# Down projection on fp16 pairs, scaled by powers of two per tile and unit, with a third copy of its weights

## The reference

```python
FFN_HIDDEN = ((8 * D_MODEL + 3 * 256 - 1) // (3 * 256)) * 256      # 2816, 22 tiles of 128

def swiglu(h, w_gate, w_up, w_down):
    return (jax.nn.silu(h @ w_gate) * (h @ w_up)) @ w_down

x = x + ga_f * swiglu(modulate(rms_norm(x, g_ffn), sh_f, sc_f), w_gate, w_up, w_down)
```

## Time and profile before

| | us |
|---|---|
| median of 3 runs | 1775.1 (1769.41 to 1775.48) |
| the profiled execution | 1775.53 |
| its span, first to last instruction | 1773.7 |
| TensorE busy | 1669.4 (94%) |
| VectorE busy | 962.2 (54%) |
| GpSimd busy | 784.9 (44%) |
| ScalarE busy | 662.7 (37%) |
| mean granted TensorE clock | 0.979 of full |

### The profile page before, as it was taken

The page is one execution under the profiler, slowest core; times in us unless marked ns, Lnnn a source line. Parts: engine busy times, 40 slices in busy tenths (PEclk is TensorE's granted clock), DMA queues, the critical chain, the costliest instruction groups (busy, mean ns, idle before and its releaser), DMA issues.

```text
span 1773.7 us, 27789 instructions
## 1 busy us (share of the span) xinstructions
PE 1669.4 (94%) x10959; PEld 1230.3 (69%) x10959; DVE 962.2 (54%) x1715; ACT 662.7 (37%) x1218; POOL 784.9 (44%) x576
## 2 busy tenths in 40 slices
PE   7999989978989999999899999997988999999998
PEld 3688878867856678666776687886776645645647
DVE  3534499895468851686418844457996522112112
ACT  3222378874143220333013113226875354153130
POOL 2144445653524452345414342551334558368363
PEclk9999999999989999999999998998999899999999
DMA  9345453313134513344225422654003224333332
GB/s 318 49 117 142 124 136 93 90 49 86 34 95 123 151 60 95 96 140 145 65 78 176 148 69 48 148 130 109 16 1 95 72 77 124 86 103 99 83 84 83
DMA packets 317279, 179.11 MB, mean 101 GB/s; under 512 B 88526, under 2 KB 310494, under 8 KB 317150
## 3 DMA queue, kind: packets, MB, share of 16 engines
q1 hardware_dynamic: 284542, 143.63, 30.9%
q10 hardware_dynamic: 32608, 33.71, 6.1%
HBM read 158.97 MB, written 2.83 MB: 91 GB/s over the span
## 4 chain that ended last, share of the span: by engine, by line
PE 60%; DVE 5%; POOL 2%; issue 2%; ACT 2%; SPq 1%; DMA 1%; ACTq 0%; DVEq 0%; POOLq 0%
PE acc L892 55%; PE small L1168 1%; DVE act L1619 1%; DVE stat L1781 1%; DVE prob_t L1795 1%; DVE scaled_ffn L1633 1%; POOL split_w L656 1%; SPq L534 1%; PE side L1073 1%; ACT prob_t L1420 0%; POOL pair_w L764 0%; PE mod_ps L989 0%; DMA inv_rows<-inv_row 0%; PE side L882 0%; DVE o_sum L1807 0%
## 5 line engine op out<-in xcount | busy, mean ns | idle before, releaser
L892 PE MATMUL acc<-act,pair_w 128*128 128x512 f16 x3168 | 580.5, 345 | 7.3 <-ACT act L1284 4.2
L892 PEld LDWEIGHTS acc<-act,pair_w 128*128 128x128 f16 x3168 | 307.5, 98 | 270.1 <-DVE act L1619 10.1
L892 PE MATMUL acc<-act,split_w 128*128 128x512 f32 (+1 forms) x1920 | 376.4, 354 | 9.9 <-DVE act L1881 4.6
L892 PEld LDWEIGHTS acc<-act,split_w 128*128 128x128 f32 x1920 | 306.4, 189 | 63.1 <-DVE act L1881 6.8
L892 PE MATMUL acc<-hidden,split_w 128*128 128x512 f32 (+1 forms) x1584 | 310.4, 357 | 10.7 <-issue 6.3
L892 PEld LDWEIGHTS acc<-hidden,split_w 128*128 128x128 f32 x1584 | 261.9, 190 | 56.6 <-issue 7.1
L653 POOL TENSOR_SCALAR split_w<-raw_w 128x1024 fp32r<-128x1024 f32 (+1 forms) x120 | 125.6, 1047 | 383.0 <-PE acc L892 292.8
L656 POOL TENSOR_TENSOR split_w<-raw_w,split_w 128x1024 fp32r<-128x1024 f32 (+1 forms) x120 | 279.2, 2327 | 10.0
L761 POOL TENSOR_SCALAR pair_raw<-pair_raw,weight_scale 128x1024 f32<-128x1024 f32 x88 | 106.1, 1205 | 357.9 <-ACT pair_w L1469 357.9
L1944 DVE SCALAR_TENSOR_TENSOR mod_acc<-mod_chunk,silu_c,mod_acc 128x256 f32<-128x256 f32 x280 | 228.1, 857 | 4.0
L1644 DVE SCALAR_TENSOR_TENSOR x_t<-acc,mod,x_t 128x512 f32<-128x512 f32 x96 | 60.3, 658 | 253.6 <-PE acc L892 253.1
(11 more groups left out here) (188 smaller groups left out, 1837.0 us busy)
## 6 DMA issues: line engine op xcount, KB each, us to landing
mod_chunk<-in_w_mod ACTq DMA_DIRECT2D x28, 1024.0 KB, 5.4
pair_raw<-in_w_gate SPq DMA_DIRECT2D x44, 512.0 KB, 4.0
pair_raw<-in_w_up SPq DMA_DIRECT2D x44, 512.0 KB, 5.4
raw_w<-in_w_in SPq DMA_DIRECT2D x64, 256.0 KB, 3.8
raw_w<-in_w_down SPq DMA_DIRECT2D x32, 512.0 KB, 3.9
raw_w<-in_w_mod SPq DMA_DIRECT2D x24, 512.0 KB, 4.1
mod_start<-in_w_mod SPq DMA_DIRECT2D x8, 1024.0 KB, 12.2
ks<-q_split SPq DMA_DIRECT2D x64, 96.0 KB, 2.3
```

Source lines behind the costliest of these rows:

```text
L892: mm = pe.matmul(acc[slot][:, a:b], weights[:, part == 2, k, :], moving[:, part == 1, k, a:b], start=(k == 0 and part == 0), stop=(k == n ...
```

## The change

The down projection goes over to fp16 pairs. Its weights get their own three raw buffers (`down_raw`), four pairs (`down_w`) and four `down_low`, a third fp16 copy: the raw scaled weight times 2^-11, which multiplies the low half of `hidden` in place of the high weights. `hidden` becomes fp16. Each down unit r = (layer, chunk, j) has a power of two of its own from the sum of squares of its tile, and each hidden tile a share (`hid_share`) from the scales of its gate and up weights; the residual's gate takes them back (`down_gate`). In a chunk's last three f the units 0, 1, 2 are prepared; unit j+3 is squared and scaled in unit j. The bound of the activations takes the maximum of the gains over partitions in place of their sum, with a transpose on TensorE.

```diff
+                def split_down(ch, j):
+                    r, n = n_down(l, ch, j), CHUNKS[ch]
+                    pool.wait_ge(down_scaled, r + 1)
+                    if r >= 4:
+                        pool.wait_ge(unit_done, u_of_down(r - 4) + 1)
+                    pool.tensor_scalar(down_low[r % 4][:, 0:n, :], down_raw[r % 3][:, 0:n, :], 2.0 ** -11, 0.0, ALU.mult, ALU.add)
+                    pool.wait_ge(down_hi, r + 1)
+                    pool.tensor_tensor(down_w[r % 4][:, 1, 0:n, :], down_raw[r % 3][:, 0:n, :], down_w[r % 4][:, 0, 0:n, :],
+                                       ALU.subtract).then_inc(down_ready, 1)
...
-                    for j in range(KT):
-                        split(u_down(l, ch) + j, n)
...
+                    split_down(ch, 0)
+                    for j in range(1, KT):
+                        if f0 + n < FT and j in (1, 2):
+                            split_pair(f0 + n + j - 1, 0)
+                        split_down(ch, j)
+                        if f0 + n < FT and j in (1, 2):
+                            split_pair(f0 + n + j - 1, 1)
...
+            def sum_down(r):
+                pe.wait_ge(down_sq, r + 1)
+                if r:
+                    pe.wait_ge(down_bits, r)
+                high = down_sum[:, r % 4:r % 4 + 1].bitcast(BF16)[:, 1:2]
+                pe.matmul(side[:, 0:1], ones16[:, :], high, start=True, stop=True).then_inc(down_ps, 1)
...
+                        if f >= f0 + n - 3:
+                            sum_down(n_down(l, ch, f - (f0 + n - 3)))
...
-                        pe.wait_ge(split_ready, ring_of[u] + 1)
+                        pe.wait_ge(down_ready, r + 1)
                         pe.wait_ge(resid, 32 * l + KT * (ch + 1) + j - 1)
+                        def down_tile(k):
+                            if j == 0:
+                                hidden_tile(k)
+                            if k == n - 1 and j + 3 < KT:
+                                sum_down(r + 3)
...
+                def square_down(ch, j, l=l):
+                    r, n = n_down(l, ch, j), CHUNKS[ch]
+                    sc.wait_ge(down_in[r % 3], 16 * (r // 3 + 1))
...
+                def round_down(ch, j, l=l):
+                    r, n = n_down(l, ch, j), CHUNKS[ch]
+                    sc.wait_ge(down_scaled, r + 1)
...
+                def last_downs(k):
+                    if k >= 1 and k + 2 < KT:
+                        round_down(len(CHUNKS) - 1, k + 2)
+                    if k + 3 < KT:
+                        square_down(len(CHUNKS) - 1, k + 3)
...
                         if f + 2 < FT:
                             square_pair(f + 2)
+                        if f >= f0 + n - 3:
+                            square_down(ch, f - (f0 + n - 3))
...
                         if f + 2 < FT:
                             round_pair(f + 2)
+                        if f >= f0 + n - 3:
+                            round_down(ch, f - (f0 + n - 3))
+                    if ch < len(CHUNKS) - 1 or l == DEPTH - 1:
+                        for j in range(3, KT):
+                            square_down(ch, j)
+                            round_down(ch, j)
...
+                def scale_down(ch, j):
+                    ve.wait_ge(down_ps, r + 1)
...
+                    ve.scalar_tensor_tensor(out=raw, in0=raw, scalar=down_scale[:, 2:3],
+                                            in1=hid_share[:, 0:n].rearrange("p (k a) -> p k a", a=1).broadcast_to((P, n, P)),
+                                            op0=ALU.mult, op1=ALU.mult).then_inc(down_scaled, 1)
...
                         product(f)
+                        if f == f0 + n - 3:
+                            share_hidden(ch)
+                        if f >= f0 + n - 3:
+                            scale_down(ch, f - (f0 + n - 3))
...
-                            residual(j % 2, x_t[:, j, :], l, mod[:, l, 5 * KT + j, :], w)
+                            residual(j % 2, x_t[:, j, :], l, down_gate[:, n_down(l, ch, j) % 4, :], w)
+                            if j + 3 < KT:
+                                scale_down(ch, j + 3)
```

More of the change, by code:

```diff
@@ L303, in trunk @@
         prod = place("prod", [P, TOK], F32, c0 + 3072)
+        down_raw = [place("down_raw0", [P, 8, P], F32, b0 + 24576)] + raw_w
+        down_low = [place(f"down_low{i}", [P, 8, P], F16, where)
+                    for i, where in enumerate((b0 + 28672, b0 + 30720, c0 + 10240, c0 + 12288))]
+        down_w = [place(f"down_w{i}", [P, 2, 8, P], F16, b0 + 32768 + 4096 * i) for i in range(4)]
+        squares_down = place("squares_down", [P, 8 * P], BF16, norm_at + 2 * 4 * TOK)
         squares_out = place("squares_out", [P, 8 * P], BF16, c0 + 22528)
@@ L403, in trunk, with n_down, u_of_down @@
             ring += [(u_out(ll) + j, 6) for j in range(KT)]
-            ring += [(u_down(ll, ch) + j, 1) for ch in range(len(CHUNKS)) for j in range(KT)]
         ring_of = {u: r for r, (u, _) in enumerate(ring)}
+        def n_down(l, ch, j):
+            return (l * len(CHUNKS) + ch) * KT + j
+        def u_of_down(r):
+            return u_down(r // (len(CHUNKS) * KT), r // KT % len(CHUNKS)) + r % KT
         def landed(u):
@@ L630, in _ @@
                         load_pair(f)
-                    for j in range(KT):
+                        if f == f0 + n - 2:
+                            for j in range(3):
+                                load_down(ch, j)
+                    if f0 + n < FT:
+                        load_pair(f0 + n)
+                        load_pair(f0 + n + 1)
+                    for j in range(3, KT):
                         load_down(ch, j)
-                        if j < 2 and f0 + n < FT:
-                            load_pair(f0 + n + j)
             for t in range(4):
@@ L891, in dense_tile @@
                     for a, b in ((0, 512), (512, TOK))[:1 if w == LAT else 2]:
-                        mm = pe.matmul(acc[slot][:, a:b], weights[:, part == 2, k, :],
+                        own = low[:, k, :] if low is not None and part == 1 else weights[:, part == 2, k, :]
+                        mm = pe.matmul(acc[slot][:, a:b], own,
                                        moving[:, part == 1, k, a:b],
@@ L1298, in _ @@
                 sc.activation(root_first[:, :], eps[:, 0:1], ACT.Sqrt)
-                squares(2 * l, TOK, ready)
+                squares(2 * l, TOK, ready, last_downs if l else None)
                 def take_rows(i):
```

124 lines of the change are left out of this document (92 added, 32 removed).

## The result

The changed kernel takes 1813.0 us (median of 4 runs, 1811.3 to 1814.2); the kernel before, beside it, 1774.7 us (4 runs). The ratio is 1.0221, 95% interval 1.0199 to 1.0244: slower by some 39 us. The forecast was 1808 us, range 1783 to 1832.

The account below looks back on a forecast made before the run. TensorE, busy 94% of 1773.7 us, bounds the kernel. Rests of +10.9 (layer 0) and +15.4 (layer 1), clock +5, sums +1.4 make +32.7 on 1775.5, the 22.8 gain already inside: 1808 us, range 1783 to 1832.

Parts of the forecast that it names:

- (a): Likeliest case: TensorE waits for the added scaling and square chain in both layers' down phases; 1808 us, 70%.
- The format's gain: Down matmuls in fp16: 11.0 us less in layer 0, 6.4 in layer 1, 5.4 from four buffers; together -22.8.
- The chain per unit: Down units 1 to 4, residual to square: layer 1 short by 0.6 us, its last chunk by 1.1; layer 0 passes.
- Unit 1 of layer 0: TensorE waits for the square's sum before unit 1's last tile; first chunk rests 8 us, until 658.8.
- Unit 0 of layer 0: Sum for unit 3 in down unit 0: rest of 3.7 us forecast in layer 1's first chunks, none in layer 0.
- The scaling: VectorE's scaling of a 128x1024 down tile: 1.2 us taken, bounds 0.96 and 3.3 if it meets a GpSimd subtraction.
- rival (d): VectorE's scaling and GpSimd's subtraction collide in most chains, costing 2 us more in each of those units: 1838 us, 12%.
- Silu in layer 1: First two chunks: ScalarE, held at the rounding of unit 0, gives silu late to the next gate; 2.2 us each.
- The clock: Lower clock behind TensorE's rests: 2.8 us per layer 0 chunk, 5 in all for layer 1, bounds 0 and 14.
- Costed at nothing: Semaphores, maximum for the bound, later sums, extra scale operations, weight loads lie beside TensorE's work; layer 1's attention part: 0.

Follow-up runs that it names:

- e10_fp16_spread: e6_fp16_alone, with the late-modulation sums of the last f of layer 0's first two chunks spread over down units 0 to 3: 1742.8 us, 0.9832.
- e6_fp16_alone: Kernel before, with down weights and `hidden` as unscaled fp16 pairs made by GpSimd, two buffers, no third copy: 1757.3 us, 0.9906.
- e1_ahead: Changed kernel, with ScalarE's square of down unit r+1 put ahead of its rounding of unit r: 1787.2 us, 1.0088.
- e3_both: e1_ahead, with the sums of even and odd down units in two PSUM banks: 1782.5 us, 1.0065.
- e7_spread: e3_both, with the late-modulation sums of each layer 0 chunk's last f spread over down units 0 to 3: 1768.3 us, 0.9969.
- e5_const: Changed kernel without squares and sums for the down units, each scaled by the same constant power of two: 1777.7 us, 1.0033.
- e9_after_spread: Changed kernel, with the late-modulation sums of each layer 0 chunk's last f spread over down units 0 to 3: 1790.4 us, 1.01.
- e11_later_add: e8_all, with TensorE's last late-modulation sum in layer 0 after down unit 5 instead of 4, VectorE's addition behind residual 6: 1758.0 us, 0.9922.
- e8_all: e7_spread, with ScalarE's roundings of down units 0 and 1 moved behind silu, each one f later: 1766.7 us, 0.9962.

## Why the prediction was right, step by step

The forecast is 5 us under the measurement, and its likeliest case, (a), is what happened: the chain residual, small operations, scaling, rounding, square, sum reaches round to TensorE's own queue. That it came so close is in part errors that cancel. On the span, layer 0's down phases cost 5.1 us more than forecast (16.0 against 10.9), layer 1's three chunks 3.0 less (17.4 against 15.4 and 5 for the clock), everything else 1.8 more (3.2 against 1.4).

- *The format's gain* was right in the stream: a down unit takes 7.8 us in layer 0; layer 1's last down phase is 31.3 us in e10_fp16_spread against 33.0, 1.8 less (forecast 1.9). All of it together, 22.8 us, is never seen: e6_fp16_alone gives 17, since the two rests on GpSimd per layer 1 chunk stay with two buffers (0.93 and 1.18 us) and layer 0's late residual takes some. The kernel as changed has the four buffers, and in its place the other rests.
- *The chain per unit.* Forecast short by 0.6 us in layer 1 and 1.1 in the last chunk; measured 0.39 and 0.99. The 1.6 us for unit 1 in layer 1 did not come in either chunk, the 1.3 for unit 2 only in the first (1.26, then 0.40), so a chunk's rests are 6.4 and 5.5 us and not 7.8. Layer 0's later units pass, as forecast.
- *Unit 1 of layer 0.* Sum forecast at 658.8, came at 658.23. This closeness is luck. The phase began 1.7 us earlier than in the kernel before (634.44 instead of 636.10), so counted from its start the sum came 23.8 us in and not 22.7; the scaling ahead of the late sums took 3.18 us and not 1.2. The forecast's own terms, too, put the residual at 653.1 (653.04 + 2.25 - 2.15) and not at 653.6. The cause of the rest has three parts, by experiment: the square behind the rounding (e1_ahead: the rest goes from 6.81 to 5.05), the single PSUM column (e3_both: to 3.99), the late sums in front of the residual (e7_spread: to none).
- *Unit 0 of layer 0* is the term that was missing. I counted it for layer 1 alone (3.7, measured 4.36), but the sum for unit 3 also rests 2.01, 2.57 and 3.84 us in layer 0's three chunks. This is the main part of the 5.1 us that the three chunks came out above the forecast. Not all of the 8.4 us adds, since unit 1's rest ends when VectorE is through, whenever it began (6.81 us instead of 8).
- *The scaling* was the disputed price: 1.2 taken, 0.96 to 3.3 as bounds. It is 1.28 alone, up to 3.18 when it meets a subtraction, mean 1.79. This made unit 0's chain long in layer 0's first two chunks (3.18 us at 638.03 and at 844.32) and, with the two-column operation of 1.97 us, in layer 1's (1.88 at 1518.62). In layer 0's third chunk it is 1.02 us for six tiles; there the last product itself stood behind late sums until 1016.69. The 32 large scalings together took 16 us more than without collisions, not all of them in a chain that TensorE waits for, and rival (d), 1838 us, did not come.
- *Silu in layer 1*: forecast 2.2 us a chunk; the gate/up phases of the first two chunks are 2.0 us longer. ScalarE is late as forecast, held by VectorE's scaling (2.61 us at 1495.53), but TensorE meets this first at the square's sum (0.86 us at 1502.60) and then at silu (0.48 at 1503.26), before the gate unit of the chunk's last f.
- *The clock.* I gave 2.8 us to each chunk of layer 0 and 5 in all to layer 1. The windows of the changed kernel (us, busy of TensorE, of its loads, of VectorE, ScalarE and GpSimd, granted clock, DMA) behind the rests of 2.01, 6.81, 4.36 (twice) and 2.46 us:

```profile
643.43:650.98 7.55, 7.55 (x48) 4.58 (x49) 7.55 (x10) 0.00 (x0) 4.58 (x3) 1.00 0.25 69
...
658.23:663.20 4.97, 4.97 (x17) 2.34 (x18) 2.70 (x7) 0.00 (x0) 1.11 (x1) 0.50 0.37 106
...
1522.73:1529.60 6.87, 6.87 (x25) 2.76 (x26) 2.97 (x6) 2.10 (x3) 6.79 (x4) 0.75 0.27 76
...
1658.20:1665.10 6.90, 6.90 (x21) 2.63 (x22) 3.42 (x6) 1.85 (x2) 6.82 (x4) 0.62 0.26 76
1767.70:1771.80 4.10, 4.07 (x19) 1.69 (x19) 2.33 (x6) 0.76 (x2) 1.50 (x2) 1.00 0.33 96
```

  Of the rests in layer 1 the two of 4.36 us cost something, that of 2.46 us nothing: 6.87 x 0.25 and 6.90 x 0.38, 4.3 us. In layer 0 the losses are 2.5 (4.97 x 0.5), about 2.8 and, in the third chunk, where two rests of 3.84 and 3.52 us each bring the clock down, 4.9.
- *Costed at nothing*: layer 1's attention part took 3.2 us more. 1.8 us of it is one rest of TensorE at 1168.13 on VectorE's `inv_tok`, which the kernel before does not have: VectorE's `q_split` before it took 2.64 us; in the kernel before that one took 1.31, and the next, behind `inv_tok`, 2.78. So a long hold by GpSimd's subtraction (2.69 us at 1164.72) seems to have moved to the other side of `inv_tok`; that is argued from the durations, not tried. The other 1.4 us stay open.

What the added work is worth by itself, from the ladder of ratios: changed kernel 1.0221, minus the ScalarE order 1.0088, minus the shared column 1.0065, minus squares and sums 1.0033, minus scaling, third copy and ScalarE's rounding 0.9906. That is 24, 4, 6 and 22 us, together the 39 lost and the 17 that the format alone gives; the last step also goes back to two buffers, so it holds a loss as well. The 28 us of the last two steps are roughly the price of the added work, the other 28 that of its places in queues. The division is not sharp: e5_const still rests 4.05, 6.18 and 4.28 us on residual 0 of layer 0's chunks, where e6_fp16_alone rests 3.04, 5.72 and 0.88. Nor do the gains of single moves add up: e1_ahead (24 us) and e9_after_spread (21) both shorten unit 1 of layer 0, and behind the first two moves the spread was worth 17. With all the moves tried (e11_later_add) the changed kernel comes to 1758 us, and the unscaled one to 1743. Of these 15 us, 9 lie in layer 1's first two down phases (48.5 against 43.9 us each), where TensorE rests on `hidden`, on GpSimd's halves and on the square's sums (2.44, 1.52, 0.64, 1.07 and 0.45 us in the first), and 5 between layer 0's last down phase and layer 1's first, which stay open.

The Trainium skill, page "SBUF — State Buffer", section "Who interferes with whom", says that of a VectorE and a GpSimd instruction that contend, the first to issue has the shared ports for its whole length. The rows agree in both directions: the scaling at 638.03, just behind GpSimd's subtraction of 638.00, took 3.18 us for 1.28, and the subtraction at 1519.52 took 2.97 for 2.13 behind the scaling of 1518.62.

## What to carry to other kernels

A producer's chain that runs through four engines must be laid against the time that one unit lasts, in the first unit above all, and in each queue the step that depends on nothing late (here the square) belongs in front of the one that does. Mending one such place gave back 24 of the 39 us; it was visible as ScalarE idle for 12.74 us in front of a square whose operand had landed. And before a format is made safe by work on every tile, time the format without it: here it was worth 17 us alone and 30 us once the late sums no longer stood before the first residual, and what kept it safe cost 56 us as first placed and still 15 us with the best places found.

## What the runs showed of the hardware

- VectorE operations of one or two columns were held as long as large ones: 1.65, 1.97 and 1.98 us where 0.15 to 0.17 is usual, with GpSimd in a subtraction, and 1.00 and 1.06 us for 0.23 to 0.29 beside its scaled copy of 1.12 us. In e8_all three held in turn made a chain of six small ones last 5.1 us (1481.24 to 1486.30). Why so small an operation is held at all is not shown.
- GpSimd pays too: beside VectorE's scaling its own scaled copy of 1024 columns took 2.09 us and its subtraction 2.97, for 1.12 and 2.13.
- In the changed kernel the granted clock stayed at 2.4 GHz behind TensorE's rests of 2.01, 2.46 and 2.57 us and was halved to 1.2 GHz for some time behind those of 3.52, 3.84, 4.36, 6.81 and 8.22 us; in e6_fp16_alone it was halved behind 3.04 us. The loss did not grow with the rest: 1.7 us behind the 3.04 us (six units in 48.5 instead of 46.8), 1.7 and 2.6 behind the two of 4.36, 2.8 behind the 8.22 us (the window 865.93 to 872.50 at 0.57).
- Rests of 2.0 to 2.6 us are not safe either, and their length alone does not tell. Two rests of the same length and place, in layer 1's first and second chunk, came out differently: 2.03 and 2.02 us in e1_ahead (first two rows), 2.62 us twice in e5_const (last two). The columns are those of the windows above; the granted clock is the third number from the end:

```profile
1510.65:1515.00 4.35, 4.35 (x14) 1.72 (x15) 3.32 (x7) 2.23 (x4) 4.35 (x3) 0.62 0.00 0
1642.35:1647.00 4.65, 4.65 (x23) 2.17 (x24) 3.32 (x7) 2.53 (x4) 4.65 (x3) 1.00 0.00 0
...
1509.37:1513.00 3.63, 3.63 (x10) 1.37 (x11) 1.03 (x1) 1.06 (x1) 3.55 (x2) 0.59 0.51 144
1640.48:1646.00 5.52, 5.35 (x24) 2.26 (x24) 1.15 (x2) 1.06 (x1) 5.44 (x4) 1.00 0.32 95
```

  So that the changed kernel's short rests cost nothing was in part chance.
